# Delta rule: the L2 norms of queries and keys taken out of the vectors and put into scalar factors

## The reference

```python
def _l2norm(x):
    return x * lax.rsqrt(jnp.sum(x * x, axis=-1, keepdims=True) + NORM_EPS)   # NORM_EPS = 1e-6

def _gated_delta_chunkwise(q, k, v, beta, g):
    q = q * (dk ** -0.5)
    ...
    kk = jnp.einsum('cbhtd,cbhsd->cbhts', kc, kc)
    a_mat = jnp.where(strict, bc[..., :, None] * kk * decay_mat, 0.0)
    lhs = a_mat + jnp.eye(CHUNK)
    sol = triangular_solve(lhs, rhs, lower=True, unit_diagonal=True)
    qk = jnp.einsum('cbhtd,cbhsd->cbhts', qc, kc) * decay_mat
    ...

# in the layer
dq, dk_, dv_ = jnp.split(_causal_conv_silu(dn_qkv, dn_conv_w), 3, axis=-1)
dq, dk_ = _l2norm(_heads(dq, DN_HEADS)), _l2norm(_heads(dk_, DN_HEADS))
h_b = _rmsnorm(_gated_delta_chunkwise(dq, dk_, dv_, beta, g), dn_norm_w)
h_b = _merge_heads(h_b) * jax.nn.silu(dn_z)
```

## Time and profile before

| | us |
|---|---|
| runs before (3) | 1913.25, 1913.93 (median), 1915.49 |
| span of the profiled execution (the page gives no other time of it) | 1913.3 |
| PE busy | 1895.3 |
| DVE busy | 1398.8 |
| ACT busy | 947.8 |
| POOL busy | 344.2 |
| mean granted TensorE clock | 0.997 |

### The profile page before, as it was taken

One profiled execution on the slowest core, in us unless ns is written; L12 is line 12 of the kernel. 1 busy time (PEld: TensorE's weight loads), 2 busy tenths in 40 slices (PEclk: granted clock), 3 DMA queues, 4 the chain that ended last, 5 costly groups with the idle time before them and its releaser, 6 DMA issues.

```text
span 1913.3 us, 27611 instructions
## 1 busy us (share of the span) xinstructions
PE 1895.3 (99%) x10948; PEld 1638.9 (86%) x10948; DVE 1398.8 (73%) x1970; ACT 947.8 (50%) x1409; POOL 344.2 (18%) x543
## 2 busy tenths in 40 slices
PE   8999999999999999999999999999999999999998
PEld 8989999878888999988888888888888888888886
DVE  5686777676989888989989768665465686657675
ACT  6556566654544333444445465554444455544544
POOL 1025344351122222223223200000000000111000
PEclk9999999999999999999999999999999999999999
DMA  7455454555788877777888857755556543544563
GB/s 257 133 167 176 122 172 137 155 160 172 262 274 286 271 257 239 238 261 241 298 284 300 305 200 231 230 181 184 191 173 209 176 131 123 182 151 149 181 229 132
DMA packets 209744, 393.16 MB, mean 205 GB/s; under 512 B 13000, under 2 KB 62448, under 8 KB 208208
## 3 DMA queue, kind: packets, MB, share of 16 engines
q1 hardware_dynamic: 191248, 323.17, 51.6%
q0 software_dynamic: 18224, 68.17, 11.3%
q10 hardware_dynamic: 144, 0.07, 0.0%
HBM read 387.13 MB, written 4.23 MB: 205 GB/s over the span
## 4 chain that ended last, share of the span: by engine, by line
PE 94%; DVE 2%; ACT 2%; issue 1%; DMA 0%; SPq 0%; DVEq 0%; ACTq 0%
PE GB L2152 53%; PE GB L2179 18%; PE GB L2164 9%; PE GB L2167 5%; PE SB L415 1%; PE SB L1723 1%; PE SB L1715 1%; PE SB L819 1%; PE SB L784 1%; PE SB L1822 1%; PE SB L1829 1%; PE SB L1179 1%; ACT WH L2071 1%; DVE WL L2076 0%; DMA xin<-in_x 0%
## 5 line engine op out<-in xcount | busy, mean ns | idle before, releaser
L2076 DVE TENSOR_TENSOR WL<-raw,WH 128x1024 fp32r<-128x1024 f32 x605 | 732.3, 1237 | 197.4 <-ACT WH L2071 196.4
L2071 ACT ACTIVATE WH<-raw 128x1024 fp32r<-128x1024 f32 x605 | 621.7, 1057 | 320.5 <-PE GB L2152 227.1
L2152 PE MATMUL GB<-WH,uHL 128*128 128x512 f32 x1792 | 484.9, 392 | 0.0
L2152 PEld LDWEIGHTS GB<-WH,uHL 128*128 128x128 f32 x1792 | 333.3, 188 | 68.1 <-issue 0.5
L2179 PE MATMUL GB<-uHL,WH 128*128 128x256 f32 x2048 | 294.9, 287 | 1.6 <-DVE uHL L451 1.6
L2152 PE MATMUL GB<-WH,hHL 128*128 128x512 f32 x1024 | 279.5, 395 | 0.0
L2152 PE MATMUL GB<-WL,uHL 128*128 128x512 f32 x896 | 276.0, 389 | 0.0
L2179 PEld LDWEIGHTS GB<-uHL,WH 128*128 128x128 f32 x2048 | 265.6, 192 | 6.2 <-issue 3.4
L2152 PEld LDWEIGHTS GB<-WH,hHL 128*128 128x128 f32 x1024 | 190.6, 188 | 41.1 <-issue 2.7
L1409 DVE SCALAR_TENSOR_TENSOR macc<-wm,csil,macc 128x512 f32<-128x512 f32 x300 | 209.3, 745 | 2.8 <-DMA wm<-in_w_mod 1.7
L2152 PEld LDWEIGHTS GB<-WL,uHL 128*128 128x128 f32 x896 | 168.2, 188 | 35.4
(11 more groups left out here) (403 smaller groups left out, 1968.3 us busy)
## 6 DMA issues: line engine op xcount, KB each, us to landing
raw<-in_w_in SPq DMA_DIRECT2D x512, 512.0 KB, 4.6
raw<-in_w_out SPq DMA_DIRECT2D x96, 512.0 KB, 5.0
wm<-in_w_mod POOLq DMA_DIRECT2D x64, 512.0 KB, 5.5
wm<-in_w_mod POOLq DMA_DIRECT2D x64, 256.0 KB, 4.2
xin<-in_x SPq DMA_DIRECT2D x4, 512.0 KB, 5.7
E<-decay_rows POOLq DMA_DIRECT2D x4, 512.0 KB, 4.2
hres<-in_x POOLq DMA_DIRECT2D x1, 2048.0 KB, 10.8
cin<-in_ctx POOLq DMA_DIRECT2D x1, 2048.0 KB, 11.3
```

Of the source, the lines that this page charges most:

```text
L2071: e.activation(place(s)[0][:, :, :], raw[s % NR][:, :, :], ACT.Copy).then_inc(*wh.inc("WH", s))
L2076: e.tensor_tensor(low[:, :, :], raw[s % NR][:, :, :], f32(high[:, :, :]), sub).then_inc(*wl.inc("WL", s))
L2152: m = e.matmul(banks[j][:, :], x[:, c, 128 * j:128 * j + 128], w[:, k, :], start=i == 0 and k == 0 and n == 0, stop=i == 7 and k == 1 and ...
```

## The change

The norms are no longer applied to the vectors. The scores are computed from unscaled queries and keys.
- Keys: in `decayed_dve`, ahead of each pair's L842, VectorE takes the sums of squares from the diagonal of the keys' scores (four tensor_tensor_reduce with the identity), adds 1e-6, takes the reciprocal, and multiplies by beta and by -1; these factors replace beta in L842 and in `quad_dve`. GpSimd takes the inverse square root (`factors_pool`), which scales the values in `values_of_act`.
- Queries: ScalarE still squares, but TensorE sums with eight products whose moving operand is one column of ones, so that the sum lies along the partitions of the tokens; it enters the norm of the output as its epsilon (`norms_pool`).
- Ln, Exp with their table loads, the GpSimd products and the keys' squares are gone. The turns of the queries' norm move (`CONVS`), and `scores_pe` waits for the convolution's product instead of L796's.

```diff
-CONVS = (1, 2, 3, 4, 5, 6, 10, 12, 13, 16)
+CONVS = (1, 2, 3, 4, 5, 6, 7.5, 9, 10, 10.5)
...
-            e.reciprocal(colBe[:, :, :], colBe[:, :, :]).then_inc(*g_dve.inc("b2"))
-            e.wait_ge(*g_dve.at("b2"))
-            e.tensor_scalar(colNB[:, :, :], colBe[:, :, :], -1.0, None, mul).then_inc(*g_dve.inc("be"))
+            e.reciprocal(colBe[:, :, :], colBe[:, :, :]).then_inc(*g_dve.inc("be"))
...
-            if kind < 2:
-                m = 2 * n + kind
+            if kind == 0:
                 yield
                 e.wait_ge(*cv_dve.at("dst", r))
...
-                e.activation(sq[:, :, :], taken(kind, n), ACT.Square).then_inc(*l2_act.inc("sq", m))
-                yield
-                yield
-                e.wait_ge(*l2_pe.at("s", m))
-                for b in range(2):
-                    e.activation(sq[:, 2 * b:2 * b + 2, :], SB[2 + b][:, :], ACT.Ln,
-                                 bias=eps[:, 0:1]).then_inc(*l2_act.inc(f"ln{b}", m))
-                e.wait_ge(*l2_act.at("ln1", m))
-                e.activation(sq[:, :, :], sq[:, :, :], ACT.Exp, scale=-0.5).then_inc(*l2_act.inc("ex", m))
+                if n:
+                    e.wait_ge(*l2_pe.at("s", n - 1))
+                e.activation(sq0[:, :, :], taken(kind, n), ACT.Square).then_inc(*l2_act.inc("sq", n))
+                yield
+                yield
+                e.wait_ge(*l2_pe.at("s", n))
+                e.activation(ssq[:, n, :, :], SB[3][:, 0:8].rearrange("p (i h) -> p i h", i=2), ACT.Identity,
+                             bias=eps[:, 0:1]).then_inc(*l2_act.inc("ss", n))
...
-                for b in range(2):
-                    claim(e, bank, 2 + b, l2_act.at(f"ln{b}", m))
-                    t = e.matmul(SB[2 + b][:, :], ones[:, :], squares[m % 2][:, 2 * b:2 * b + 2, :], start=True, stop=True,
-                                 skip_group_check=True)
+                claim(e, bank, 3, l2_act.at("ss", n))
+                for i in range(2):
+                    for h in range(4):
+                        t = e.matmul(SB[3][:, 4 * i + h:4 * i + h + 1], sq0[:, h, 128 * i:128 * i + 128], ones[:, 0:1],
+                                     start=True, stop=True, skip_group_check=True)
...
-                e.wait_ge(*l2_act.at("ex", m))
-                e.tensor_tensor(taken(kind, n), taken(kind, n), squares[m % 2][:, :, :], mul).then_inc(*l2_pool.inc("n", m))
+        def factors_pool(e, n):
+            for h in range(0, 4, 2):
+                e.wait_ge(*l2_dve.at(f"i{h}", n))
+                e.tensor_tensor(kinv[:, n, :, h:h + 2], ssk[:, n, :, h:h + 2],
+                                power[:, 0:4].rearrange("p (i h) -> p i h", i=2), ALU.pow).then_inc(*l2_pool.inc(f"f{h}", n))
                 yield
...
-                    e.wait_ge(*l2_pool.at("n", 2 * n + 1))
+                    e.wait_ge(*cv_dve.at("dst", 3 * n + 1))
...
+                    e.wait_ge(*g_dve.at("be"))
+                if h % 2 == 0:
+                    hs = slice(h, h + 2)
+                    for g in (h, h + 1):
+                        for i, s in enumerate((SB[SCORE_BANKS[g]][:, 256:384], half(SB[2], g % 2)[:, 128:256])):
+                            v = e.tensor_tensor_reduce(out=tsc[:, 256 * (g % 2) + 128 * i:256 * (g % 2) + 128 * i + 128], in0=s, in1=ident[:, :], scale=1.0, scalar=0.0, op0=mul,
+                                                       op1=add, accum_out=ssk[:, n, i, g:g + 1])
+                    v.then_inc(*l2_dve.inc(f"s{h}", n))
+                    e.wait_ge(*l2_dve.at(f"s{h}", n))
+                    e.tensor_scalar(ssk[:, n, :, hs], ssk[:, n, :, hs], 1e-6, None, add).then_inc(*l2_dve.inc(f"e{h}", n))
+                    e.wait_ge(*l2_dve.at(f"e{h}", n))
+                    e.reciprocal(ssk[:, n, :, hs], ssk[:, n, :, hs]).then_inc(*l2_dve.inc(f"i{h}", n))
+                    e.wait_ge(*l2_dve.at(f"i{h}", n))
+                    e.tensor_tensor(kbe[:, n, :, hs], ssk[:, n, :, hs], colBe[:, :, 4 * n + h:4 * n + h + 2],
+                                    mul).then_inc(*l2_dve.inc(f"b{h}", n))
+                    e.wait_ge(*l2_dve.at(f"b{h}", n))
+                    e.tensor_scalar(knb[:, n, :, hs], kbe[:, n, :, hs], -1.0, None, mul).then_inc(*l2_dve.inc(f"n{h}", n))
+                    e.wait_ge(*l2_dve.at(f"n{h}", n))
+                if h == 0:
                     e.wait_ge(*qe_act.at("E", n))
...
-                e.activation(vt[:, i], SB[1 + i][:, :], ACT.Copy).then_inc(*qv_act.inc(f"v{i}", n))
+                for h in range(4):
+                    a = e.activation(vt[:, i, h], SB[1 + i][:, 128 * h:128 * h + 128], ACT.Copy, scale=kinv[:, n, i, h:h + 1])
+                a.then_inc(*qv_act.inc(f"v{i}", n))
...
+            e.wait_ge(*l2_act.at("ss", n))
+            e.tensor_scalar(ssq[:, n, :, :], ssq[:, n, :, :], 4e-6, None, mul).then_inc(*qs_pool.inc("e", n))
             e.wait_ge(*qs_act.at("s13", n))
-            e.tensor_scalar(rq[:, n, :, :], rq[:, n, :, :], 4.0 / 128, 4e-6, mul, add).then_inc(*qs_pool.inc("v", n))
+            e.tensor_scalar(rq[:, n, :, :], rq[:, n, :, :], 4.0 / 128, None, mul).then_inc(*qs_pool.inc("m", n))
+            e.wait_ge(*qs_pool.at("e", n))
+            e.wait_ge(*qs_pool.at("m", n))
+            e.tensor_tensor(rq[:, n, :, :], rq[:, n, :, :], ssq[:, n, :, :], add).then_inc(*qs_pool.inc("v", n))
...
-            be = [colBe[:, i, 4 * n:4 * n + 4].unsqueeze(2).to_broadcast([128, 4, 128]) for i in range(2)]
+            be = [kbe[:, n, i, :].unsqueeze(2).to_broadcast([128, 4, 128]) for i in range(2)]
```

More of the change, by code:

```diff
@@ L252, in hybrid_program @@
         rq = sb("rq", [128, 4, 2, 4])
+        ssq = sb("ssq", [128, 4, 2, 4])
+        ssk = sb("ssk", [128, 4, 2, 4])
+        kinv = sb("kinv", [128, 4, 2, 4])
+        kbe = sb("kbe", [128, 4, 2, 4])
+        knb = sb("knb", [128, 4, 2, 4])
         power = sb("power", [128, 16])
@@ L462, in hybrid_program @@
         g_act = steps("g_act", "H0", "H1", "t", "gb", "ip", "be", "me", "ml", "A", "E")
-        g_dve = steps("g_dve", "L0", "L1", "rb", "s", "sa", "ma", "b1", "b2", "be", "mb", "mq", "mc", "ms", "mr", "mp", "mo",
+        g_dve = steps("g_dve", "L0", "L1", "rb", "s", "sa", "ma", "b1", "be", "mb", "mq", "mc", "ms", "mr", "mp", "mo",
                       "f", "B", "sp", "na", "g", "rowG", "a", "M", "rowM", "x", "colA", "colEn", "colG")
@@ L697, in hybrid_program @@
         cv_dve = steps("cv_dve", *[f"{j}{sh}" for j in range(4) for sh in (1, 2, 3)], "dst")
-        l2_pe, l2_act, l2_pool = steps("l2_pe", "s"), steps("l2_act", "sq", "ln0", "ln1", "ex"), steps("l2_pool", "n")
+        l2_pe, l2_act, l2_pool = steps("l2_pe", "s"), steps("l2_act", "sq", "ss"), steps("l2_pool", "f0", "f2")
+        l2_dve = steps("l2_dve", *(x + h for h in "02" for x in "seibn"))
         qk_pe, qp_dve = steps("qk_pe", "k1", "k3"), steps("qp_dve", "p0", "p1", "p2", "p3")
@@ L705, in hybrid_program @@
         qs_act = steps("qs_act", *(f"s{i}{h}" for i in range(2) for h in range(4)))
-        qs_pool = steps("qs_pool", "v", "r")
+        qs_pool = steps("qs_pool", "e", "m", "v", "r")
         qd_act = steps("qd_act", "y5", "z5", "y6", "z6", "W")
@@ L776, in conv_pe @@
             n, kind = divmod(r, 3)
[L777 to L779 removed]
+            if kind == 0:
+                for _ in range(7):
                     yield
[L781 to L796 removed]
+                e.wait_ge(*l2_act.at("sq", n))
+                claim(e, bank, 3, l2_act.at("ss", n))
[3 more added lines that the diff above has]
+                                     start=True, stop=True, skip_group_check=True)
+                t.then_inc(*l2_pe.inc("s", n))
+                yield
+        def factors_pool(e, n):
[3 more added lines that the diff above has]
+                                power[:, 0:4].rearrange("p (i h) -> p i h", i=2), ALU.pow).then_inc(*l2_pool.inc(f"f{h}", n))
                 yield
@@ L836, in decayed_dve @@
                         e.wait_ge(*qd_pe.at("o1", n - 1))
-                nb = [colNB[:, i, 4 * n + h:4 * n + h + 1] for i in range(2)]
+                nb = [knb[:, n, i, h:h + 1] for i in range(2)]
                 for o, s, c, f in ((PT[:, h, 0:256], a[:, 0:256], sc, E[:, h, 0:256]),
@@ L869, in values_of_act @@
                 e.wait_ge(*qv_pe.at(f"t{i}", n))
-                if i == 0 and n:
-                    e.wait_ge(*qd_dve.at("R", n - 1))
-                e.activation(vt[:, i], SB[1 + i][:, :], ACT.Copy).then_inc(*qv_act.inc(f"v{i}", n))
+                if i == 0:
+                    e.wait_ge(*l2_pool.at("f2", n))
+                    if n:
+                        e.wait_ge(*qd_dve.at("R", n - 1))
+                for h in range(4):
+                    a = e.activation(vt[:, i, h], SB[1 + i][:, 128 * h:128 * h + 128], ACT.Copy, scale=kinv[:, n, i, h:h + 1])
+                a.then_inc(*qv_act.inc(f"v{i}", n))
             yield
@@ L2368, in _ @@
             stages["attan"] = attended_a_pool(e)
```

(2 more changed lines are left out.)

8 lines of the change are left out of this document (2 added, 6 removed).

## The result

| | before | after |
|---|---|---|
| median of the runs, us | 1913.93 (1913.25 to 1916.21, 5 runs) | 1920.45 (1920.28 to 1921.32, 5 runs) |
| ratio, with its 95% interval | | 1.0034 (1.0022 to 1.0046) |
| span of the profiled execution, us | 1913.3 | 1919.5 |

The changed kernel is 0.34% slower, 6.5 us; the interval of the ratio lies clear above 1. Forecast were 1920.5 us, and slower with a chance of 0.63.

The account below looks back on a forecast made before the run. TensorE, busy 99%, was taken as the bound. Group 0's 3.95 us, groups 1 and 2's 0.38 and group 3's 2.54 made +6.9 on the 1913.3 span, 1920.2, stated as 1920.5; range 1914.3 to 1925.

Parts of the forecast that it names:

- X: VectorE's four reduces, four small operations and the handover to L842, put ahead of each pair's eight L842: 2.2 us.
- The signs named beforehand: TensorE waits at second pairs (some 2 us, 5.5 in group 0), clock then under 1.0, 2 us split wait near 440.
- One sign of being wrong: On VectorE ahead of L842: the forecast is wrong if the reduces are far from 0.28 us each.
- one-column block: The queries' eight TensorE products with one moving column: 1.85 us a group in place of 1.70.
- group 0, second pair later by: TensorE's second pair of scores in group 0 comes X + 0.15 later: 2.35 us.
- group 0, the clock: After 5.5 us idle in group 0 TensorE's clock falls to 1.2 GHz: 1.6 us lost.
- groups 1 and 2, each: Wait of 2.04 us, less the keys' block 1.70, less 0.3 at L946, plus 0.15: +0.19 us.
- group 3: Wait of 2.04 us, less 1.70, plus 0.15, plus 2.05 for the late split behind the inverse: 2.54 us.
- the rival that frees VectorE early: Group 0's L842 follows the first scores instead of waiting until 124.22: only +1.4 us, 1914.7; chance 0.15.
- the wait at L946: TensorE's wait for VectorE's L1039: 0.3 us won ahead of groups 1 and 2 each, nothing ahead of group 3.
- The base: The profiled span of 1913.3 us, with the runs' median taken as 0.6 us above it.
- The covered chain: Rival: VectorE's added work at the second pairs and the inverse's delay stay hidden, giving 1904.9 us; chance 0.08.

Follow-up runs that it names:

- e3: The changed kernel with six products of ones by 512 columns filling group 0's gap ahead of its second pair of scores: 1918.69 us, ratio 1.0021.
- e1: The kernel before with only the queries' half of the change, the keys keeping their L784 block, Ln, Exp and GpSimd product: 1914.41 us, ratio 1.0003.
- experiment 6: The changed kernel with VectorE's work reordered, four L856 (old L842) between the small dependent operations and colNB kept as before: 1917.44 us, ratio 1.0018.
- experiment 9: The changed kernel with second pair a slot later, VectorE's chain interleaved, and the pair's first product ahead of the claim of SB2: 1909.09 us, ratio 0.9973.
- experiment 5: Not a run's number here: the 5 is us between executions of e7, the changed kernel with the second pair a slot later (1912.67 to 1917.92 us).
- e10: The same kernel as e7 run again for a second profile and more executions: 1916.12 us median, profiled execution 1914.52 us.
- e7: The changed kernel with the second pair of scores, its L856 (old L842) and the diagonal copies one slot later: 1916.75 us, ratio 1.0015.
- e8: The kernel before with VectorE's added reduces and small operations alone, their results unused, both L784 blocks kept: 1925.35 us, ratio 1.0062.
- e11: The kernel of e7 with three products of ones by 512 columns filling group 0's gap of 2.8 us: 1914.09 us, ratio 1.0001.

## Why the prediction was right, and where its steps were off

The mechanism was the forecast one: TensorE loses four blocks of 1.70 us and waits for X at every second pair, plus a fallen clock in group 0 and a late inverse in group 3. The signs named beforehand came: the waits at the second pairs, the fallen clock, the late split. One sign of being wrong came in part: the reduces take 0.21 us each and not 0.28. The terms, head set aside:

| term | forecast | measured | by |
|---|---|---|---|
| X | 2.2 | 1.78 | the timeline after |
| one-column block | 1.85 | 1.78 | 162.13 - 159.39 - 0.96, below |
| group 0, second pair later by | 2.35 | 1.86 | table |
| group 0, the clock | 1.6 | 2.68 | table, e3 |
| groups 1 and 2, each | +0.19 | -0.10 | table |
| group 3 | 2.54 | 3.15 | table |
| sum | 6.9 | 7.5 | |

The total came out well because errors cancelled, and that is luck. With X and the one-column block as measured, my own sum gives 4.4 us (group 0 1.86 + 1.6, groups 1 and 2 -0.30 each, group 3 1.56). The 3.1 us that it lacks are 1.1 of clock, 0.4 in groups 1 and 2, and 1.6 in group 3.
- **X was mis-sized.** I took 0.28 a reduce, between 0.20 and 0.49; it was 0.21, and the accumulator's record of 0.08 us stands beside the next reduce, not between them. Behind the reduces I counted five steps of 0.20 us; there are four, and 0.12 us ahead of the first. The Trainium skill, "VectorE: DVE Perf Modes", section "Two Vector instructions with no wait between them", says that such an operation is two instructions; the trace shows both (DVE_READ_ACCUMULATOR2_ANT, 0.08 us), and the second is nearly free in a stream.
- **The one-column block** took 1.78 us, for 1.85 forecast. TensorE in group 1's queries:

```profile
159.39 1.84 PE L782 MATMUL SB<-ones,sq 128*128 128x1 f32 x16
161.10 1.20 PE L2202 MATMUL GB<-uHL,WH 128*128 128x256 f32 x8
162.13 0.64 PE L2202 MATMUL GB<-uHL,WL 128*128 128x256 f32 x4
```

  That is 0.111 us a record, the same as L919's with 128 columns, so the number of moving columns does not count here. By the Trainium skill, "TensorE: Matmul & The Clock Gate", section "LDWEIGHTS (loading the stationary operand)", 16 loads are 1.71 us by its figure; the trace is 4% above. The replacement wins nothing, as said, and e1 puts it at +0.36 us in all.
- **Group 0.** VectorE began 1.2 us earlier than forecast (122.99 for 124.22), but that is the head's 1.30, which all engines had; the rival that frees VectorE early is refuted. The clock's term failed in size: I charged 24 records at the low level, 1.6 us; it stayed low for the whole second pair (4.90 us for 2.47) and a little beyond, and e3 measures 2.67.
- **Groups 1 and 2.** The stall was 1.55 us (2.04 forecast), and the two pairs of group 1 are 7.17 us apart for 5.45 before, 1.72 more: in a stream a product starts before the record of the last one ends, and behind a gap it does not. The block is gone (-1.70), and the wait at L946 fell from 0.41 to 0.15 us (-0.26, 0.3 forecast). About 0.15 comes behind the pair, 0.08 of it the one-column block. Together -0.09. The smaller X and block alone would have made -0.30 of my sum; 0.17 of the 0.2 between them is that overlap. At group 3 the same wait grew by 0.1 us, so L946 gave 0.4 in all.
- **Group 3** was right in cause and short by 1.6 us of what X leaves. I let the split behind the inverse be late, with a cover of 0.3 us. The triangular product itself waits for the same inverse, with a cover of about 1.4 us (438.02 less 435.73 and half of 1.80), and that I did not see; but it adds nothing, since the two waits end with one and the same inverse: in experiment 6 the wait at L899 is gone and the one for the split is still 1.2 us. What I lacked is its length. The inverse came 6.3 us later: 3.2 for TensorE's lag at the second pair, 1.8 for X, and 1.3 because the substitution took 36.5 us from L1074 (405.55) for 35.2 before (400.57 to 435.73). So it was 3.1 us later against TensorE, and less the cover of 0.3 that is the two waits of 1.68 and 1.20. I had taken the substitution's length as fixed.
- **The base.** I took the profiled execution to lie 0.6 us below the median. In the later runs, where time and span of one execution are both known, the time is mostly the span plus 1.8 us (1921.32 for 1919.5), so it more likely took 1915.1, 1.2 above the median, with its slow head. That is an estimate; its own time is not on record. The changed kernel's profiled execution was 0.9 above its own median. So the usual execution loses 6.5 us by the change, where these two show 7.5, and my sum of 6.9 lies between.

The covered chain, which I gave 0.08 as the way to be faster, is what experiment 9 builds, at 1909.1 us; for the code as changed TensorE waited at every second pair.

## What to carry to other kernels

Moving work from the busiest engine (PE, 99%) to a less busy one (DVE, 73%) pays only if the receiver is not on a handover that the first engine waits for: look at what is queued between the producer's end and the claim of the next bank, here a cover of 0.16 us for 1.8 us of new work. Before giving up such a change, move the waiting product (one slot later, or the part of it whose bank is free ahead of the wait) and put independent operations between dependent small ones: the same arithmetic went from 6.5 us slower to about 5 us faster, 1.3 of it by the order alone. And compare executions by the start of the same instruction in both traces, with the head set aside, since executions of one and the same kernel lie up to 3 us apart, and in one experiment 5; 1.3 to 1.7 us of that was a clock that fell ahead of the changed stage.

## What the runs showed of the hardware

- The clock can fall to 1.2 GHz after a TensorE gap of 2.81 us and can hold through the same gap in another execution of the same program (e10 and e7: 0.87 and 1.00 in 120 to 130 us). In group 0 it fell in all profiled executions with gaps of 3.2 us and more (0.66 in 130 to 135 us in e8), and held in those with 1.2 (e9) and 1.47 us (before, 1.00). But a short gap is not safe: at group 3's inverse it fell behind a wait of 1.70 us in e9 and of 2.36 in e11 (0.83 in 430 to 440 us in both), and held behind 1.68 us in the changed kernel and 2.36 in e7 and e10 (1.00 there). The Trainium skill, "TensorE: Matmul & The Clock Gate", section "What's actually happening", says of a kernel's first products that how many of them run at the low clock varies between runs of one kernel; these runs show the same chance behind a gap in the middle. So the gap of 2.81 us cost between 0 and 1.7 us on top.
- GpSimd's steps of the substitution take about four times as long in some stretches as in others. GpSimd and VectorE in the changed kernel:

```profile
428.86 1.16 POOL L1108 TENSOR_TENSOR TB<-NB,XB 128x64 f32<-128x64 f32 x1
...
430.50 1.18 POOL L1108 TENSOR_TENSOR TB<-NB,XB 128x75 f32<-128x75 f32 x1
431.76 0.35 POOL L1111 TENSOR_TENSOR XB<-XB,TB 128x75 f32<-128x75 f32 x1
```

```profile
430.17 1.33 DVE L2099 TENSOR_TENSOR WL<-raw,WH 128x1024 fp32r<-128x1024 f32 x1 [0.31 <-ACT WH L2094]
```

  The long step at 430.50 lies beside a split (430.17 to 431.50), and behind it the steps are short. So do all steps from 424.90 to 430.02, beside four splits (424.89 to 429.86). The longest step of all is the first, in the same two timelines:

```profile
407.83 5.53 POOL L1108 TENSOR_TENSOR TB<-NB,XB 128x31 f32<-128x31 f32 x1 [2.66 <-DVE NB L1074]
```

```profile
407.52 5.73 DVE L2099 TENSOR_TENSOR WL<-raw,WH 128x1024 fp32r<-128x1024 f32 x5
```

  One step lasts as long as the five splits beside it. In the kernel before five steps of 1.00 to 1.11 us lie beside the same five splits (402.54 to 408.48), so the changed kernel is four steps behind, and at 0.24 to 0.3 us for a short step that is most of the 1.3 us by which its substitution is longer. So the length of a substitution depends on which splits fall beside it and how: 35.1 to 36.5 us in group 3 over the traces with the pair where it was, 34.4 to 34.7 with the pair a slot later. That the splits are the cause is read from such places and was not tried, and the profile's times of GpSimd are rough.
